# A two-layer hybrid decoder step: one small product moved to another pair of banks, the first weights loaded in two halves, the last norm factor spread by products with the unit matrix

## What is computed

```python
def rms_norm(x, g):
    xf = x.astype(jnp.float32)
    y = xf * lax.rsqrt(jnp.mean(xf * xf, axis=-1, keepdims=True) + NORM_EPS)
    return (y * g.astype(jnp.float32)).astype(x.dtype)

h = rms_norm(x, norm_g) @ w_in
...
def phi(rows, pe, w1, w2):
    blk = rows[:, idx] + pe[None, None, :, None, :]
    flat = jnp.moveaxis(blk, 3, 2).reshape(b, n_cmp, g, CMP_LEN * hd)
    return jax.nn.silu(flat @ w1) @ w2
...
s = jnp.einsum('bqgrd,bngd->bqgrn', q, kc).astype(jnp.float32) * SCALE
p_cmp, _ = masked_softmax(s, valid_c, -1)
imp = jnp.einsum('bqgrn,nm->bqgm', p_cmp, ov)
...
y = merge_branches(...)                    # gate and up projections, product with w_out
return x + y
...
y_prompt = rms_norm(xp, final_norm_g)
```

## Time and profile before

| | |
|---|---|
| median of 3 executions | 952.19 us (951.5 to 952.32) |
| the profiled execution | 952.22 us |
| its span on the core | 950.6 us |
| TensorE busy | 924.8 us, 97% of the span |
| DVE, ACT, POOL busy | 655.4, 461.1, 187.5 us |
| the chain that ended last | TensorE 91%, DVE 4%, ACT 2%, issue 2%, DMA 1% |

### The profile page before, as it was taken

One profiled execution on the slowest core, in us unless ns is written; L12 is line 12 of the kernel. 1 busy time (PEld: TensorE's weight loads), 2 busy tenths in 40 slices (PEclk: granted clock), 3 DMA queues, 4 the chain that ended last, 5 costly groups with the idle time before them and its releaser, 6 DMA issues.

```text
span 950.6 us, 21757 instructions
## 1 busy us (share of the span) xinstructions
PE 924.8 (97%) x8064; PEld 860.5 (91%) x8064; DVE 655.4 (69%) x1483; ACT 461.1 (49%) x877; POOL 187.5 (20%) x321
## 2 busy tenths in 40 slices
PE   6999999999999999999999999999999999999996
PEld 6999988988888799999999999889988878999996
DVE  6999657667665567656769976665765564775574
ACT  6344746555443444334544456555554425443352
POOL 2100000226558400000000000003574662000000
PEclk9999999999999999999999999999999999999998
DMA  9672975636969874333666577646369799435421
GB/s 346 255 251 108 419 281 200 243 124 221 289 208 288 252 295 188 144 134 119 247 249 241 217 275 289 267 159 274 141 201 290 231 262 324 172 134 185 170 90 50
DMA packets 66201, 209.89 MB, mean 221 GB/s; under 512 B 12192, under 2 KB 49760, under 8 KB 56112
## 3 DMA queue, kind: packets, MB, share of 16 engines
q1 hardware_dynamic: 57056, 187.67, 54.2%
q0 software_dynamic: 8896, 20.81, 7.0%
q10 hardware_dynamic: 144, 0.01, 0.0%
HBM read 202.48 MB, written 41.36 MB: 257 GB/s over the span
## 4 chain that ended last, share of the span: by engine, by line
PE 91%; DVE 4%; ACT 2%; issue 2%; DMA 1%; DVEq 0%; SPq 0%; ACTq 0%
PE bank L1010 64%; PE bank L1217 8%; PE bank L1023 5%; PE bank L1137 3%; PE bank L1115 3%; PE bank L1251 1%; PE bank L1347 1%; PE bank L1150 1%; PE bank L1319 1%; PE bank L1278 1%; DVE short L1639 1%; DMA big<-in_w_tok 1%; DVE paged_r L1880 1%; PE bank L1232 0%; ACT qTC_high L1542 0%
## 5 line engine op out<-in xcount | busy, mean ns | idle before, releaser
L1702 DVE TENSOR_TENSOR big_r<-big,paged_r 128x1024 fp32r<-128x1024 f32 x160 | 195.5, 1225 | 81.4 <-ACT paged_r L1464 79.8
L1010 PE MATMUL bank<-xnT_high_r,paged_r 128*128 128x288 f32 x768 | 231.7, 302 | 0.0
L1010 PE MATMUL bank<-xnT_r,paged_r 128*128 128x288 f32 x704 | 207.7, 295 | 0.0
L1010 PE MATMUL bank<-xnT_high_r,big_r 128*128 128x288 f32 x704 | 207.0, 294 | 0.0
L1010 PE MATMUL bank<-short_r,big_r 128*128 128x288 f32 x576 | 170.8, 296 | 0.0
L1464 ACT ACTIVATE paged_r<-big 128x1024 fp32r<-128x1024 f32 x160 | 167.1, 1051 | 6.5 <-DMA big<-in_w_feat 4.2
L1010 PEld LDWEIGHTS bank<-xnT_high_r,paged_r 128*128 128x128 f32 x768 | 144.1, 188 | 7.0 <-issue 5.3
L1010 PE MATMUL bank<-short_r,paged_r 128*128 128x288 f32 x448 | 134.2, 300 | 9.4 <-DVE big_r L1702 9.4
L1010 PE MATMUL bank<-kvp_r,paged_r 128*128 128x288 f32 x448 | 133.7, 298 | 0.0
L1010 PEld LDWEIGHTS bank<-xnT_high_r,big_r 128*128 128x128 f32 x704 | 132.5, 188 | 0.0
L1010 PEld LDWEIGHTS bank<-xnT_r,paged_r 128*128 128x128 f32 x704 | 132.3, 188 | 0.0
(11 more groups left out here) (333 smaller groups left out, 1830.8 us busy)
## 6 DMA issues: line engine op xcount, KB each, us to landing
big<-in_w_tok SPq DMA_DIRECT2D x13, 2048.0 KB, 9.2
big<-in_w_feat SPq DMA_DIRECT2D x12, 2048.0 KB, 8.4
big<-in_w_gate SPq DMA_DIRECT2D x10, 2048.0 KB, 9.1
out_kept_dil<-in_cache_dil SPq DMA_DIRECT2D x16, 1020.0 KB, 13.1
paged<-in_pool SPq DMA_DIRECT2D x218, 64.0 KB, 4.6
big<-in_w_up SPq DMA_DIRECT2D x12, 1024.0 KB, 8.7
paged<-in_pool POOLq DMA_DIRECT2D x166, 64.0 KB, 5.0
big<-in_kv_win SPq DMA_DIRECT2D x4, 2048.0 KB, 8.8
```

Of the source, the lines that this page charges most:

```text
L1010: last = mm(out, l, r, start=(c == 0 and i == 0), stop=(c == n - 1 and i == 2))
L1702: v.tensor_tensor(l_part, full, h_part.bitcast(FP32), ALU.subtract).then_inc(*split_done.inc(s))
```

## The change

It has four parts.

1. The compressed keys (`kc`, both halves) and the first block sum (`("impsum", 0)`) take a bank of the TR pair in place of PJ; their readers on ACT and DVE release it there.
2. In the list of steps `("sturn", 0, "slc1")` and `("vc", 1)` change places.
3. The first weight block is loaded in two halves of 4 tiles each, the first half between the first and the second pair of x, and ACT and DVE round and split it in two instructions each (new step `firsthalf` after two `start` steps). For the first product TensorE takes each half by itself: the eight products with the rounded weights, which wait for the rounding alone, then the four with the low part of the weights.
4. DVE no longer forms `diag`: TensorE takes the column of reciprocals, read as if it stood in all 128 columns, as its weights and multiplies it by the unit matrix.

```diff
@@ steps
-            ("imp", 1), ("spv", 0, "cnew"), ("vc", 1), ("sturn", 0, "slc1"), ("impsum", 1)] + splits(("gate", 0, 0), 0) + \
+            ("imp", 1), ("spv", 0, "cnew"), ("sturn", 0, "slc1"), ("vc", 1), ("impsum", 1)] + splits(("gate", 0, 0), 0) + \
@@ program_steps
-    out = sum(starts[0:4], []) + halves(0, 0) + sum(starts[4:], []) + [(0, ("square", 0))] + halves(0, 1)
+    out = sum(starts[0:2], []) + [(0, ("firsthalf",))] + sum(starts[2:4], []) + halves(0, 0) + sum(starts[4:], []) + [(0, ("square", 0))] + halves(0, 1)
@@ trunk_program
+    in_turn_bank = lambda s: s[0] == "kc" or s == ("impsum", 0)
...
+    ring_for = lambda s: TR if in_turn_bank(s) else PJ
+    bank_for = lambda s: (tr if in_turn_bank(s) else pj)(s)
@@ sync
             load_x(0)
+            load_first_half(0, first_of_all_in)
             load_x(1)
-            load_first(0)
+            load_first_half(1, first_in[0])
             sp.wait_ge(x_in[0], 16)
@@ tensor, spread
-                        last = mm(tr(s)[:, P * tt:P * tt + n], ones[0:n, :], diag[0:n, P * tt:P * tt + n],
+                        last = mm(tr(s)[:, P * tt:P * tt + n], rn[0:n, tt:tt + 1].to_broadcast([n, P]), ident[0:n, 0:n],
@@ tensor, proj
+                    if (layer, s[1]) == (0, 0):
+                        for h in range(2):
+                            tiles = range(4 * h, 4 * h + 4)
+                            pe.wait_ge(*(high_done.at(("round", ("tok", 0), 0)) if h else (first_rounded, 1)))
+                            for c in tiles:
+                                pe.wait_ge(*x_split.at(("start", c)))
+                                for z in (xg_high, xg_low):
+                                    mm(pj(s)[:, 0:T], wh[:, c, :], z[:, c, :], start=(c == 0 and z is xg_high), stop=False)
+                            pe.wait_ge(*(split_done.at(("split", ("tok", 0), 0)) if h else (first_split, 1)))
+                            for c in tiles:
+                                last = mm(pj(s)[:, 0:T], wl[:, c, :], xg_high[:, c, :], start=False, stop=(c == KT - 1))
@@ tensor, kc
-                    wait(pe, PJ.is_free(s))
+                    wait(pe, TR.is_free(s))
                     for g in range(KV):
-                        last = mm(pj(s)[HD * g:HD * (g + 1), 0:256], w2[:, 0, :], hid[0][:, 256 * g:256 * (g + 1)],
+                        last = mm(tr(s)[HD * g:HD * (g + 1), 0:256], w2[:, 0, :], hid[0][:, 256 * g:256 * (g + 1)],
@@ scalar
+                elif k == "firsthalf":
+                    item = ("tok", 0)
+                    act.wait_ge(first_of_all_in, 16)
+                    f(high_part(item, 0)[:, 0:512], split_part(bigb(item), item, 0)[:, 0:512], ACT.Copy)\
+                        .then_inc(first_rounded, 1)
@@ vector, root
-                    link(v.reciprocal(rn, rn))
-                    for tt, n in enumerate(PARTS):
-                        last = v.tensor_scalar(diag[0:n, P * tt:P * tt + n], ident[0:n, 0:n], rn[0:n, tt:tt + 1], None,
-                                               ALU.mult)
-                    last.then_inc(*inverted.inc(s))
+                    v.reciprocal(rn, rn).then_inc(*inverted.inc(s))
@@ vector
+                elif k == "firsthalf":
+                    item = ("tok", 0)
+                    h_part, l_part, full = (split_part(z, item, 0)[:, 0:512] for z in (high(item), low(item), bigb(item)))
+                    dve.wait_ge(first_rounded, 1)
+                    v.tensor_tensor(l_part, full, h_part.bitcast(FP32), ALU.subtract).then_inc(first_split, 1)
```

41 lines of the change are left out of this document (25 added, 16 removed).

## The result

| | before | after |
|---|---|---|
| median of 20 executions each, taken together | 951.63 us | 949.72 us |
| ratio after to before, with its 95% interval | | 0.9982 [0.9976, 0.9989] |
| the profiled execution, and its span | 952.22 us, 950.6 us | 949.71 us, 947.9 us |
| TensorE's first matmul | 9.37 us | 5.58 us |
| TensorE's start of product 1 (the second block) | about 14.7 us | 14.56 us |

The change makes the kernel 1.7 us faster (0.0018 of 951.63, between 1.0 and 2.3); the forecast was 4.65 us, from 952.19 to 947.5. The time lies within the range by a hair (949.72 against 949.8), but the move is little more than a third of the forecast.

What follows compares the result with a forecast made beforehand. TensorE, busy 97% of the span, was taken as the bound. Opening 1.8, piece 6 0.0, pieces 12 and 14 1.6, swap 0.6 and spread 0.65 us sum to 4.65: 952.19 to 947.5 us, range 945.0 to 949.8.

## What to carry to other kernels

A start that is made earlier is worth only what stands behind it is early too: ask of each transfer that follows the one you split when it is first used in the new order, and give it a bound from both sides, above all if the old order hid its lateness, as here where halving the load alone cost nothing. A wait taken away comes back at the next step that needs the same slow engine, and a step that is moved has to be followed to its reader as well as to its producer, since the reader holds the bank. Where stretches at half clock come and go between executions, read one offset at a fixed instruction in each record, and take the device time from many executions.

## What the runs showed that I had not expected

- One more transfer among the first five left the DMA engines less busy (share 0.82 and 220 GB/s for 1.06 and 357 between 6 and 8 us) and brought the fourth pair of x in at 10.3 to 11.0 us instead of 8.1 to 9.1, and block 1 at 11.5 to 12.4 instead of 10.1 to 11.4, whichever queue it was in; three more cost no more than one, and 256 more packets nothing.
- The time of this kernel follows its granted clock from execution to execution: over 123 executions of the kernel before, time and mean clock correlate with -0.83, 0.49 us for each 0.001 of mean clock. The 1.5 us wait moved to `o_sb` goes with a mean lower by 0.0018 in the kernel with only `kc` 0 moved, which makes 0.9 of the 1.1 us by which it came out slower.
